# Moving part of a second attention ahead of a routing step, and its probability scaling to ScalarE

## The reference, cut to what matters

```
for i in range(DEPTH):                                   # DEPTH = 2
    h = modulate(rms_norm_2(x, norm1_gain[i]), sh1, sc1)
    q, k, v = project_qkv(h, w_qkv[i], ...)              # 8 query heads, 2 key heads
    ...
    o = latent_global_attention(...) if i == 0 else latent_window_attention(...)
    x = x + g1 * (o @ w_o[i])
    ...
    h2 = modulate(rms_norm_2(x, norm2_gain[i]), sh2, sc2)
    x = x + g2 * peer_ffn(h2, peer_w_q[i], peer_sub_keys[i], peer_u[i], peer_v[i])

def attend_block(qblk):                                  # 128 query rows, 512 keys
    s = jnp.einsum('bqgrd,bkgd->bgrqk', qblk, ka).astype(jnp.float32) * scale
    p = jax.nn.softmax(s, axis=-1)
    return jnp.einsum('bgrqk,bkgd->bqgrd', p.astype(va.dtype), va)

def peer_block(hb, w_q, sub_keys, u_tab, v_tab):         # 128 tokens
    q = (hb @ w_q).reshape(n, PEER_HEADS, PEER_QDIM)
    s1, s2 = (q's two halves against the 128 sub keys)
    v1, i1 = lax.top_k(s1, PEER_TOPK)
    v2, i2 = lax.top_k(s2, PEER_TOPK)
    top_s, pos = lax.top_k(v1[..., :, None] + v2[..., None, :], PEER_TOPK)
    expert = ...
    w = softmax(top_s) * gelu(einsum(u_tab[expert], hb))
    return jnp.einsum('nhk,nhkd->nd', w, v_tab[expert])
```

## Time and profile before

| | us |
|---|---|
| median of 3 runs (lowest, highest) | 3102.56 (3101.69, 3106.98) |
| the profiled execution, its own time | 3107.37 |
| its span, first to last instruction | 3105.6 |
| PE busy | 2565.4 (83%) |
| DVE busy | 2229.3 (72%) |
| POOL busy | 1221.3 (39%) |
| ACT busy | 626.3 (20%) |
| mean DMA rate | 331 GB/s |
| mean granted TensorE clock | 0.943 |

### The profile page before, as it was taken

The page is one execution under the profiler, slowest core; times in us unless marked ns, Lnnn a source line. Parts: engine busy times, 40 slices in busy tenths (PEclk is TensorE's granted clock), DMA queues, the critical chain, the costliest instruction groups (busy, mean ns, idle before and its releaser), DMA issues.

```text
span 3105.6 us, 29770 instructions
## 1 busy us (share of the span) xinstructions
PE 2565.4 (83%) x9452; PEld 1617.2 (52%) x9452; DVE 2229.3 (72%) x5499; ACT 626.3 (20%) x1743; POOL 1221.3 (39%) x1028
## 2 busy tenths in 40 slices
PE   6798786899896679997849898788878898977777
PEld 2677664688785567884524343333335443333222
DVE  0438978699878777776678888875644698887655
ACT  1221212200012121001322222322223321221111
POOL 0001543555664345662324454333410245454431
PEclk8899898999998799998979999999999999999999
DMA  9426975899998569996559999999951799999997
GB/s 391 158 95 222 342 286 203 318 356 388 403 342 334 200 229 374 409 409 250 197 204 414 419 420 413 419 420 399 400 236 57 310 418 419 420 420 420 420 420 306
DMA packets 210092, 1029.41 MB, mean 331 GB/s; under 512 B 23472, under 2 KB 25264, under 8 KB 143632
## 3 DMA queue, kind: packets, MB, share of 16 engines
q0 software_dynamic: 147456, 805.37, 65.3%
q1 hardware_dynamic: 61200, 217.61, 18.4%
q10 hardware_dynamic: 1280, 4.54, 0.4%
HBM read 1022.25 MB, written 5.18 MB: 331 GB/s over the span
## 4 chain that ended last, share of the span: by engine, by line
PE 37%; DVE 28%; DMA 26%; issue 3%; POOL 2%; ACT 2%; SPq 0%; DVEq 0%; ACTq 0%; POOLq 0%; another core or an unknown queue 0%
DMA ctx_ring<-in_peer_uv,expert 11%; PE ps L2627 8%; PE ps L1265 5%; PE ps L2395 5%; DVE low L1455 4%; DMA w_ring<-in_weights 3%; PE ps L1183 3%; DMA w_ring<-in_peer_uv,expert 3%; PE ps L1277 2%; DMA xT<-in_peer_uv,expert 2%; DMA low<-in_peer_uv,expert 2%; DMA own<-in_peer_uv,expert 2%; PE ps L460 2%; PE ps L2078 2%; DVE ctx_ring L1458 2%
## 5 line engine op out<-in xcount | busy, mean ns | idle before, releaser
L2627 PE MATMUL ps<-own,consts_sb 128*128 128x512 f32 x736 | 350.8, 609 | 60.7 <-ACT consts_sb L2867 60.7
L2360 POOL DMA_INDIRECT own<-in_peer_uv,expert x184 | 208.1, 1131 | 464.8 <-PE ps L2627 321.6
L1438 POOL DMA_INDIRECT ctx_ring<-in_peer_u,ctx_expert x124 | 160.0, 1290 | 422.5 <-DVEq L1956 248.8
L1265 PE MATMUL ps<-mix,w_ring 128*128 128x256 f32 x1408 | 308.2, 382 | 11.1 <-DVE mix L406 11.1
L1265 PEld LDWEIGHTS ps<-mix,w_ring 128*128 128x128 f32 x1408 | 270.1, 192 | 49.3 <-issue 11.9
L3036 DVE SCALAR_TENSOR_TENSOR own<-own,htok 128x1024 f32<-128x1024 f32 x184 | 224.4, 1222 | 75.1 <-DMA own<-in_peer_uv,expert 72.0
L1438 POOL DMA_INDIRECT ctx_ring<-in_peer_v,ctx_expert x148 | 190.0, 1284 | 206.1 <-DVE low L1455 157.9
L2627 PEld LDWEIGHTS ps<-own,consts_sb 128*128 128x128 f32 x736 | 136.1, 192 | 248.5 <-issue 139.3
L2395 PE MATMUL ps<-w_ring,hT 128*128 128x512 f32 (+1 forms) x480 | 229.2, 592 | 22.7 <-DVE hT L403 15.3
L2627 PE MATMUL ps<-w_ring,consts_sb 128*128 128x512 f32 x404 | 196.6, 621 | 55.2 <-ACT consts_sb L2867 55.2
L2862 ACT ACTIVATE consts_sb<-consts_sb 128x2 f32<-128x2 f32 x256 | 52.1, 203 | 866.3 <-DVE consts_sb L3019 866.2
(11 more groups left out here) (476 smaller groups left out, 4842.4 us busy)
## 6 DMA issues: line engine op xcount, KB each, us to landing
w_ring<-in_weights SPq DMA_DIRECT2D x392, 512.0 KB
own<-in_peer_uv,expert POOLq DMA_INDIRECT x184
ctx_ring<-in_peer_v,ctx_expert POOLq DMA_INDIRECT x148
ctx_ring<-in_peer_u,ctx_expert POOLq DMA_INDIRECT x124
ctx_more<-in_peer_v,ctx_expert POOLq DMA_INDIRECT x108
w_ring<-in_peer_uv,expert POOLq DMA_INDIRECT x101, 28.8
consts_sb<-in_consts SPq DMA_DIRECT2D x1, 1536.0 KB, 10.1
ctx_ring<-in_peer_uv,expert POOLq DMA_INDIRECT x91
```

Source lines behind the costliest of these rows:

```text
L1265: ins = pe.matmul(m.ps[:, GU[j % 4], part * SEQ:(part + 1) * SEQ], w[:, k, (j % 2) * P:(j % 2 + 1) * P], m.hT[:, k, 0:SEQ], start=(k == 0) ...
L1438: pool.indirect_dma_start(out=self.slot(r), out_offset=None, in_=expert_tables(self.d)[v], in_offset=bass.IndirectOffsetOnAxis(ap=m.ctx_ex ...
L2360: pool.indirect_dma_start(out=entry(e), out_offset=None, in_=table, in_offset=bass.IndirectOffsetOnAxis(ap=m.expert[:, blk, k:k + 1], axis ...
L2627: ins = pe.matmul(m.ps[:, 2 * blk + half, :], m.diag[:, e % DIAGS, :], entry(e)[:, D + half * 512:D + (half + 1) * 512], start=(k == 0), s ...
```

## The change

In the changed kernel:

- The reciprocal stays on DVE (`even`); the scaling of the probabilities, one 128x512 instruction a head, goes to ACT (`weigh`), in both blocks of both layers. ACT copies the transposed probabilities one head later and the outputs of a pair one or two heads later.
- Of `attend(1)`, three heads (`EARLY_HEADS = 3`) are placed earlier: scores of heads 0 and 1 behind the output projection of blk 0, of head 2 among the first queries; their maxima ahead of norm 2 and after the first step of the first route.
- The first queries and scores use the two `side` banks of PSUM.
- The second half of blk 1's output projection goes from e = 2 and 3 to e = 14 to 21, one matmul an entry; the first half is spread over e = 0 to 3. Additions at e = 6 and 24, norm 2 of blk 1 from e = 24. The place "queries" opens at e = 34. Query groups and their routing start later up to the fifth.
- Context rows: 121 in the feed-forward, with 3 late ones, and 37 in the latent layer; in `attend(0)` one row after even heads and two after odd ones; 4 instead of 3 after the last item.
- The mask of layer 1 is added to one block of 128 keys instead of two.
- In layer 0 the first item's matmuls wait for their own slice of the norm, not for all eight.

```diff
-LATE_ROWS = 6
+LATE_ROWS = 3
-    SECOND_SHARE = dict(in_projection=38, rwkv=50, attention=21, out_projection=19, feed_forward=116)
-    TAIL_SHARE = dict(latent=42)
+    SECOND_SHARE = dict(in_projection=38, rwkv=50, attention=21, out_projection=19, feed_forward=121)
+    TAIL_SHARE = dict(latent=37)
-QUERY_AT = {1: 4, 2: 14, 3: 30, 4: 46, 5: 62, 6: 78, 7: 94}
+OUT_AT, OUT_PARTS = {0: 0, 1: 14}, {0: 4, 1: 8}
+QUERY_AT = {1: 6, 2: 29, 3: 44, 4: 56, 5: 68, 6: 79, 7: 94}
-ROUTE_AT = {1: (14, 1), 2: (28, 2), 3: (48, 2), 4: (68, 2), ...
+ROUTE_AT = {1: (16, 1), 2: (43, 1), 3: (58, 2), 4: (73, 2), ...
+X1_AT = {0: 6, 1: 24}
+H2_AT = 24
+EARLY_HEADS = 3
...
-                opened.update(keys=..., queries=(LEAVE_AT + 4, LAST, qT_used))
+                opened.update(keys=..., queries=(OUT_AT[1] + 8 + LEAVE_AT, LAST, qT_used))
...
 # ScalarE
-                exps(0)
+                if not early:
+                    exps(blk, 0)
                 for h in range(N_HEADS):
-                    if h + 1 < N_HEADS:
-                        exps(h + 1)
-                    if h >= 3 and h % 2:
-                        copy_out(h // 2 - 1)
-                    copy_probs(h)
+                    if max(early, 1) <= h + 1 < N_HEADS:
+                        exps(blk, h + 1)
+                    if h >= early:
+                        weigh(blk, h)
+                    if h >= 4 and h % 2 == 0:
+                        copy_out(h // 2 - 2)
+                    if h:
+                        copy_probs(h - 1)
...
 # VectorE
-            attend(0, None if i else lambda h: rows.take(v, h % 2, "latent"))
+            attend(0, 0, None if i else lambda h: rows.take(v, 1 + h % 2, "latent"))
...
             item_rows(len(first) + 1)
             if not i:
-                rows.take(v, 3, "latent")
+                rows.take(v, 4, "latent")
             add_out(0, 1)
+            for h in range(2):
+                top(1, h)
             norm_rows(("h2", 0))
             norm_first_half(("h2", 0))
+            for h in range(2):
+                even(1, h)
             if not i:
                 rows.take_rest(v, "latent")
             for at in range(first_routes[0].steps):
                 first_route_step(0, at)
+                if 2 <= at + 2 < EARLY_HEADS:
+                    top(1, at + 2)
+            for h in range(2, EARLY_HEADS):
+                even(1, h)
```

More of the change, by code:

```diff
@@ L2268, in latent_layer @@
         first_queries = [(("pq", 0, 0, 0), 1), (("pq", 0, 0, 1), 1), (("sc", 0, 0, 0), 1), (("sc", 0, 0, 1), 1)]
-        fills = [(key, 2) for key in first] + gates_of(0) + scores_of(0) + outs_of(0) + first_queries + scores_of(1) + outs_of(1)
+        fills = [(key, 2) for key in first] + gates_of(0) + scores_of(0) + outs_of(0) + scores_of(1)
         for n in range(1, len(SEQUENCE)):
-            fills += queries_of(n)
+            query, score = queries_of(n)
+            fills += [(("out", 1, 0), 1), query, score, (("out", 1, 1), 1)] if n == 1 else [query, score]
             if n == 2:
@@ L2289, in latent_layer @@
         fills += halves("pqt", 0, 0) + halves("htok", 0)
-        fills += probs_of(1) + halves("h2", 1) + one(*(("pqt",) + bg for bg in SEQUENCE[1:]))
+        fills += probs_of(1) + one(("pqt",) + SEQUENCE[1]) + halves("h2", 1) + one(*(("pqt",) + bg for bg in SEQUENCE[2:]))
         if between:
@@ L2455, in out @@
                     ins.then_inc(s.o_done, 1)
-                pe.wait_ge(*turned.emptied(item_turn(("kv", 1))))
-                for h in range(2):
-                    scores(h)
+                for h in range(early, 2):
+                    scores(blk, h)
                 for h in range(N_HEADS):
-                    if h + 2 < N_HEADS:
-                        scores(h + 2)
+                    if early <= h + 2 < N_HEADS:
+                        scores(blk, h + 2)
                     if after_scores:
@@ L2495, in first_query_turn @@
             def first_query_turn(head):
-                pe.wait_ge(*wide.emptied(("pq", 0, 0, head)))
+                pe.wait_ge(*side.emptied(("pq", 0, 0, head)))
                 turn(("pqt", 0, 0, head), [temp(0, h * P, (h + 1) * P) for h in (2 * head, 2 * head + 1)])
@@ L2542, in _ @@
                     pe.wait_ge(*turned.emptied(("h1", 1, half)))
-            else:
-                for k in range(KT):
-                    pe.wait_ge(s.normed, k + 1)
             for n in range(len(first)):
@@ L2622, in _ @@
                 beside(e)
+                if e == 0:
+                    for head in range(PAIR):
+                        pe.wait_ge(*side.emptied(("sc", 0, 0, head)))
                 if e == SLOTS:
@@ L2883, in first_route_step @@
                 if at == 0:
-                    v.wait_ge(*wide.emptied(("sc", 0, 0, head)))
+                    v.wait_ge(*side.emptied(("sc", 0, 0, head)))
                 first_routes[head].part(at)
@@ L3006, in attend, with even @@
+            def even(blk, h):
+                v.wait_ge(*wide.emptied(("s", blk, h)))
+                if i:
+                    link(v.tensor_tensor(red(h, 2), red(h, 2), red(h, 3), ALU.add))
+                v.reciprocal(red(h, 2), red(h, 2)).then_inc(s.inverted, 1)
+            def attend(blk, early=0, after_head=None):
+                for h in range(early, 2):
+                    top(blk, h)
                 for h in range(N_HEADS):
-                    weigh(h)
-                    if h + 2 < N_HEADS:
-                        top(h + 2)
+                    if h >= early:
+                        even(blk, h)
+                    if early <= h + 2 < N_HEADS:
+                        top(blk, h + 2)
@@ L3108, in beside @@
             def beside(e):
-                if e in (X1_AT, X1_AT + 2):
-                    add_out(1, (e - X1_AT) // 2)
-                if e == X1_AT + 5:
+                for half in range(2):
+                    if e == X1_AT[half]:
+                        add_out(1, half)
+                if e == H2_AT + 3:
                     norm_rows(("h2", 1))
-                if e == X1_AT + 8:
+                if e == H2_AT + 6:
                     norm_first_half(("h2", 1))
```

172 lines of the change are left out of this document (93 added, 79 removed).

## The result

The changed kernel is slower: a median of 3113.2 us over 20 runs, beside 3105.5 for the kernel before (20 runs on the same chips), ratio 1.0025, 95% interval 1.0018 to 1.0032. That is 8 us more, where 40 less were forecast. The profiled execution took 3114.2 us, its span is 3112.4, the mean granted clock 0.935.

The account below looks back on a forecast made before the run. The prediction took DMA gathers to bound the kernel, with gaps behind each first route. Terms -17 - 10 - 1 - 12 = -40 took the profiled 3107.4 to 3067.4; the median, 4.8 lower, gave 3063 us, range 3041 to 3088.

Parts of the forecast that it names:

- End of the feed-forward, +8: Second feed-forward before layer 0: eight more context rows delay the addition 11.5 us, 5.9 come back, slower PE adds 2.
- an even split of two queues: Rows at the feed-forward's end: sharing about 400 GB/s evenly, a row takes 2.6 us and the step 4 us more.
- First item, -4: Layer 0's first item: matmuls waiting only for their own norm slice start up to 4.5 us earlier; 4 taken.
- Attention of blk 0, 0: Attention of blk 0, either layer: scaling on ACT costs nothing, as PE is last and hides the longer head path.
- Rows and the first route, -23: Layer 0, from norm 2 to the first route's end: rows end at +13 us, so the stretch is 23 us shorter.
- From the last gather of layer 0 to the first of layer 1: Layer 1 up to the first route's end: shorter mask and earlier scores against later exponentials and a maximum, -1 us.
- R of layer 0: End of layer 0's first route, 1586.0 us before the change; forecast 17 us earlier, from +8 - 4 + 2 - 23.
- Behind the first route, -10 and -12: After the first route in layers 0 and 1: earlier projection and faster refilling shorten the gap in gathers by 10 and 12 us.
- In the full loop, 0: Entry loops of both layers: later queries and two routings cost nothing, since some 15 us of gathers are in flight.
- the third rival: Entry loops fall behind the gathers through routing bursts, a missing place and late weights: 60 us more, 3123; chance 0.06.
- The prediction's own sign of being wrong: Among the signs of a wrong forecast: DMA share under 0.97 in the entry loops at e = 6 to 60.
- The two rivals that I had given 0.25 and 0.06: Later scaling stretches attention, 3079 or 3085 us (0.25); the entry loop falls behind the gathers, 3123 us (0.06).

Follow-up runs that it names:

- e3: The changed kernel with the probabilities scaled on DVE and copied at once, as before the change; 3097.2 us, ratio 0.9967 to the kernel before.
- e13: The changed kernel with only the query group at e = 6 multiplied with weights already there (other queries, not the reference); 3097.8 us, ratio 0.9968.
- e1: The changed kernel with the query groups at e = 6 and e = 56 multiplied with weights already there (not the reference); 3092.7 us, ratio 0.9957.
- e14: The changed kernel with only the query group at e = 56 multiplied with weights already there (not the reference); 3103.8 us, ratio 0.9989.
- e11: The changed kernel with scaling and copies as before, and query groups at e = 6 and 56 on weights already there (not the reference); 3072.6 us, ratio 0.9885.

## Why the prediction was wrong, step by step

The forecast was 3063, in a range of 3041 to 3088; measured were 3113. Two steps failed, behind the first route and in the loop.

**End of the feed-forward, +8: near, +10.** DVE's timeline:

```profile
1428.09 1.28 DVE L1455 SCALAR_TENSOR_TENSOR low<-ctx_more,ctx_weight,low 128x1024 f32<-128x1024 f32 x1 [1.28 <-DMA ctx_more<-in_peer_v,ctx_expert]
1430.65 1.28 DVE L1455 SCALAR_TENSOR_TENSOR low<-ctx_more,ctx_weight,low 128x1024 f32<-128x1024 f32 x1 [1.27 <-DMA ctx_more<-in_peer_v,ctx_expert]
1432.25 2.48 DVE L1349 TENSOR_TENSOR xT<-xT,ps 128x512 f32<-128x512 f32 x4
1440.33 0.42 DVE L1359 TENSOR_SCALAR sg<-ps 128x256 f32<-128x256 f32 x1
```

These answer to the earlier trace rows. The addition waits for rows and not for PE, at 1432.3; 1427.8 was forecast. The counts of rows (L1455 alone: DVE busy and count, clock, DMA share, GB/s) say why, first before, then in the changed kernel:

```profile
0.00:1411.00 1411.00, 266.95 (x208) 0.93 0.81 304
```
```profile
0.00:1411.00 1411.00, 264.45 (x206) 0.93 0.80 303
1411.00:1415.00 4.00, 2.57 (x2) 1.00 1.03 411
1415.00:1432.00 17.00, 10.27 (x8) 0.73 1.03 410
```

The eight extra rows took the 17 us that were forecast, 2.1 each. The missing 4 us are older: at 1411 DVE was two rows behind the kernel before, and no run shows why. The prediction also gave a sum 4 us larger, by an even split of two queues that take turns ("DMA: Bandwidth & Descriptors" of the Trainium skill, Queues, rings and completion order). Single rows do come 2.56 us apart, as that split gives, but others followed without a wait for the DMA, and the mean of the eight is 2.1. From the addition to the norm's reciprocal it took 11.5 us (1432.25 to 1443.76) where it took 17.4 (1416.33 to 1433.71), so 5.9 of the addition's 15.9 come back (3.9 of 11.5 in the forecast). PE did slow down as forecast: the squares took 5.2 us for 16 records behind 13.3 us of idle time, then 3.6.

**First item, -4: right.** From the norm's reciprocal on DVE to that of the first item's roots it took 18.2 us before (1433.7 to 1451.9) and 14.1 after (1443.8 to 1457.9).

**Attention of blk 0, 0: off by a little in layer 0.** First maximum to the next item's rows takes 39.3 us and not 37.2. In layer 1 the same stretch (2326.2 to 2363.3) is 37.1 against 38.4, with the shorter mask in it. The price of one scaling on ACT was taken from a copy, 0.60 us; it is 0.72 (row 1572.90 of ACT's timeline, L2751).

**Rows and the first route, -23: near.** The rows behind norm 2 end at 1562.3, 12.3 us behind it (13 forecast), the route ends at 1572.7. R of layer 0 is 13.3 us earlier, where -17 was forecast; of the 4 missing, 2 are the feed-forward's and 2 attention of blk 0. From the last gather of layer 0 to the first of layer 1: -0.3 (-1).

**Behind the first route, -10 and -12: this step failed, by both its halves.** The text said that PE "follows the last scaling by a copy and an output" and put the projection at R + 21.7 and the eighth gather at R + 25.2. They came at R + 30.6 and R + 34.6 (POOL's row at 1607.31, after 25.5 us of waiting), as late as before the change. In layer 1 the first entry came at R + 32.5, 4 us earlier than before; 12 were forecast for the whole step. I had added up DVE's work and left out the round trip: with the copy one head later, ACT's queue holds a copy that PE waits for behind a scaling and exponentials that wait for DVE. PE waited 14.6 us there in layer 0. Of the 9 us that the projection came too late, 5 are DVE's own waits for scores (2.65 us at 1583.73, 2.49 at 1590.62) that stand behind these products in PE's program, and the other 4 lie behind DVE's last reciprocal (R + 20.9). e3 shows the size, 18 us over both layers. The Trainium skill ("ScalarE: Activation LUTs", Rules for kernel authors) says to do multiplications on VectorE. The trace agrees for one instruction, 0.72 us on ACT against 0.49 on DVE; in the time it is 11 us with late copies, while the 3 us with copies at once are not clear of zero.

The second half: "The next query group's weights are a new wait [...] PE waits there, but gathers are in flight; I let it cost none to 3." The wait's length followed from the step's own numbers, 16 us of loading less 5, and was 9.4. The cover was assumed, and it ends with the gathers in flight: they kept the DMA full during the wait (share 1.02), but no place came free for the next ones, and the 20 us behind the wait have a share of 0.76. The gathers had restarted only 13 us before, after a gap in which the share was 0.08. e13 prices the two waits at 18 us, e1 against e14 at 10.

**In the full loop, 0: failed.** The wait at e = 56 stood in the third rival, at some 6 us, and was held against "bursts of the same size went by". Those bursts were DVE's, beside which PE and the places went on. This one stops PE for 11.7 and 9.3 us, and is worth 3 to 11 us by e1, e13 and e14. The prediction's own sign of being wrong is there: a DMA share under 0.97, namely 0.88 from 1760 to 1800 us.

**The sum.** The forecast was -40. Taking back the scaling and copies gives 18 us, and the weights' waits 21; with both gone e11 is 36 us faster than the kernel before (29 to 43 by its interval), which holds the forecast. So the rest of the sum stands as a whole, but e11 also has the scaling back on DVE, and which terms make up the 36 was not shown. The two rivals that I had given 0.25 and 0.06 both happened in part. Of the second it was the weights' waits, at 21 us; 60 were named for them, the bursts of routing and the missing place together. Each excluded the other in my list of cases, where their conditions are independent. The case "both" was missing: 3063 + 18 + 21 = 3102, and that is still 11 below what was measured; 4 of these are R of layer 0, and the rest I can't place within the intervals.

## What to carry to other kernels

When a table moves a consumer of a ring of weight slots, list for each load the time at which its slot comes free and the time at which it is needed, and compare the difference with a load's duration under the present traffic; this needs no run. "Transfers are in flight" is no cover by itself: a stall of the engine that frees the buffers shows not while it lasts but behind it, when what was in flight has landed and nothing was issued. Look for the hole there and price it by the rate; here four waits of 40 us in all left holes of some 22 us, and 21 were measured. And when an operation is moved to an idle engine, write down its queue's order with what each entry waits for: ACT was busy only a third of that stretch, and the move still cost 11 us with the late copies.

## What the runs showed of the hardware

The same eight records of the output product take 3.78 us behind a wait of PE of 7.9 or 3.7 us and 1.99 us behind one of 2.3 or 0.7. The stretch behind the wait of 3.7 us (it ended at 1594.70) shows the lower clock, 0.50, which is 1.2 GHz of 2.4:

```profile
1595.00:1600.00 5.00, 5.00 (x16) 3.95 (x15) 2.03 (x7) 0.85 (x2) 0.00 (x0) 0.50 0.01 3
```

So each of these two longer waits cost itself and then some 1.8 us more; behind the wait of 9.4 us at e = 6 four records took 3.75 us where they take 1.88. Over the 54 us behind the route the granted clock is 0.82, a mix of both levels, where it was 0.93 before. A load of 2.1 MB beside the restarted gathers took 14.6 us from issue to PE's first matmul (1615.65 to 1630.21), and the one at e = 56 21.6 us (1758.80 to 1780.36), beyond the 16 us of the earlier trace rows.
